# Expert weights of a hybrid decoder layer: nineteen slots in place of sixteen, filled in the order in which they come free, with the first pass over the experts written out

## The reference

```python
def hier_moe(h, w_rg, b_rg, w_re, b_re, w_e1, w_e3, w_e2):
    ...
    for gi in range(N_GROUPS):
        a = jnp.einsum('td,edf->tef', t, w_e1[gi])
        b = jnp.einsum('td,edf->tef', t, w_e3[gi])
        hid = jax.nn.silu(a) * b * gate[:, gi, :, None]
        y = y + jnp.einsum('tef,efd->td', hid, w_e2[gi])
    return y.reshape(B, S, D)
```

## Time and profile before

| | |
|---|---|
| median of 3 runs | 506.74 us (506.46 to 506.91) |
| the profiled execution | 506.75 us |
| its span, first to last instruction | 505.0 us |
| mean granted TensorE clock | 0.948 of full speed |
| TensorE matmuls busy | 426.5 us, 84% |
| VectorE, ScalarE, GpSimd busy | 159.5, 173.7, 157.3 us |
| moved by DMA | 163.19 MB, mean 323 GB/s |
| chain that ended last, by engine | PE 62%, DMA 24%, VectorE 4%, ScalarE 2% |

### The profile page before, as it was taken

The page is one execution under the profiler, slowest core; times in us unless marked ns, Lnnn a source line. Parts: engine busy times, 40 slices in busy tenths (PEclk is TensorE's granted clock), DMA queues, the critical chain, the costliest instruction groups (busy, mean ns, idle before and its releaser), DMA issues.

```text
span 505.0 us, 8937 instructions
## 1 busy us (share of the span) xinstructions
PE 426.5 (84%) x3772; PEld 319.0 (63%) x3772; DVE 159.5 (32%) x345; ACT 173.7 (34%) x305; POOL 157.3 (31%) x126
## 2 busy tenths in 40 slices
PE   1847998999999999999987989898849668594983
PEld 0415987999899999997965636354416244261541
DVE  0243304899692430455244011202110201102014
ACT  1235431853558276533452322130301102030122
POOL 0009894765936857997400000000000000000000
PEclk9969999998999999999997999999989979799798
DMA  8999979397598437558879699999999999999942
GB/s 295 392 364 388 281 242 387 123 342 244 182 355 257 165 112 262 185 194 287 332 286 422 254 392 424 420 421 421 420 422 421 424 422 422 422 420 422 423 197 85
DMA packets 55719, 163.19 MB, mean 323 GB/s; under 512 B 7058, under 2 KB 33924, under 8 KB 43268
## 3 DMA queue, kind: packets, MB, share of 16 engines
q1 hardware_dynamic: 50528, 159.53, 82.4%
q10 hardware_dynamic: 5156, 3.17, 2.1%
HBM read 161.64 MB, written 1.05 MB: 322 GB/s over the span
## 4 chain that ended last, share of the span: by engine, by line
PE 62%; DMA 24%; DVE 4%; SPq 3%; ACT 2%; issue 2%; POOL 1%; DVEq 0%; ACTq 0%
PE bank L1249 33%; DMA ring<-in_w_e 15%; PE bank L1558 8%; DMA mqk<-in_w_e 5%; PE bank L1570 4%; PE bank L1531 4%; DMA ring<-in_w_ada 4%; PE bank L1520 3%; PE bank L1202 3%; SPq L351 2%; SPq L339 1%; POOL ring_r L391 1%; PE bank L1604 1%; PE bank L1486 1%; ACT ring_r L426 1%
## 5 line engine op out<-in xcount | busy, mean ns | idle before, releaser
L391 POOL TENSOR_TENSOR ring_r<-ring,ring_r 128x512 fp32r<-128x512 f32 x120 | 156.9, 1345 | 87.8 <-ACT ring_r L426 87.6
L1249 PE MATMUL bank<-ring_r 128*128 128x256 f32 x832 | 111.3, 285 | 4.6 <-DVE att L815 2.3
L1249 PEld LDWEIGHTS bank<-ring_r 128*128 128x128 f32 x832 | 103.8, 191 | 7.3 <-issue 4.3
L648 ACT ACTIVATE raw<-bank,sm 128x128 f32<-128x128 f32 x72 | 27.1, 457 | 165.1 <-PE bank L1531 165.1
L426 ACT ACTIVATE ring_r<-ring 128x2048 fp32r<-128x2048 f32 x30 | 57.4, 1912 | 43.6 <-PE bank L1249 26.1
L1558 PE MATMUL bank<-ring,raw 128*32 128x256 f32 x768 | 51.9, 423 | 17.3 <-DMA ring<-in_w_e 16.9
L1558 PEld LDWEIGHTS bank<-ring,raw 128*32 128x32 f32 x768 | 28.3, 121 | 39.5 <-issue 27.8
L1127 DVE TENSOR_TENSOR tmp<-bank,tmp 128x256 f32<-128x256 f32 x8 | 3.4, 425 | 134.0 <-ACT tmp L656 134.0
L1531 PEld LDWEIGHTS bank<-const,xn 128*128 128x128 f32 x288 | 35.9, 199 | 9.0 <-issue 7.8
L1531 PE MATMUL bank<-const,xn 128*128 128x128 f32 x288 | 37.7, 286 | 1.1 <-DVE const L1078 1.1
L1202 PE MATMUL bank<-ring,sm 128*32 128x256 f32 x384 | 27.3, 434 | 12.3 <-DMA ring<-in_w_ada 12.3
(11 more groups left out here) (301 smaller groups left out, 533.3 us busy)
## 6 DMA issues: line engine op xcount, KB each, us to landing
ring<-in_w_e SPq DMA_DIRECT2D x72, 1024.0 KB, 25.9
ring<-in_w_ada SPq DMA_DIRECT2D x24, 1024.0 KB, 10.8
ring<-in_w_in SPq DMA_DIRECT2D x22, 1024.0 KB, 8.5
hT<-in_w_e SPq DMA_DIRECT2D x6, 1024.0 KB, 23.1
qkT<-in_w_e SPq DMA_DIRECT2D x6, 1024.0 KB, 25.1
gm<-in_w_e SPq DMA_DIRECT2D x6, 1024.0 KB, 26.3
mqk<-in_w_e SPq DMA_DIRECT2D x6, 1024.0 KB, 26.2
ring<-in_w_out SPq DMA_DIRECT2D x4, 1024.0 KB, 5.1
```

The lines of the kernel that those rows point to most:

```text
L391: pool.tensor_tensor(ring_r[:, slot_of(n), sl], ring[:, slot_of(n), sl], hi(d)[:, sl].bitcast(F32), ALU.subtract).then_inc(s["w_lo"], 1)
L648: ins = act.activation(xg[:, b, k, :], token_bank[:, j * P:(j + 1) * P], ACT.Identity, bias=S("B2p", KD)[:, k:k + 1], scale=S("A2p", KD)[: ...
L1249: ins = pe.matmul(out, left(k), right(k), start=(i == 0 and k == 0), stop=(i == 2 and k == nk - 1))
```

## The change

There are now nineteen slots. Two are a new tensor, `extra`; the SBUF for it comes from the reserve that the compiler object keeps for DMA descriptors (`dynamic_dma_scratch_size`), set from 16384 bytes per partition to 256. The third is the first 2048 floats of `late`, one tensor in which `osig` and most of `vaug` now lie; both are dead once `osig` has been transposed (job `ymT1`). A table `RELEASES` lists all nineteen with the job that frees each, in the order of those jobs, and the first nineteen expert units are put into the slots in that order (`ORDER`), as are all later ones. On SP the 77 further units of the first pass are now issued by straight code, unit m waiting for `used` >= m - 18, and on PE the eight quads are straight code, with constants in their waits. The further passes, which don't run here, use sixteen of the slots in loops.

```diff
-XSLOTS = SLOTS + 4
+XSLOTS = SLOTS + 7
+YSLOTS = 16
...
+def hi_slot(job):
+
+    return RING + [UNIT_JOB[n] for n in DENSE].index(job) % HI
+
+
+RELEASES = ([(SLOTS + 4, None), (SLOTS + 5, None), (SLOTS + 6, "ymT1"), (SLOTS + 1, "brm3")] + [((NPRE + u) % RING, "ada5") for u in range(4)] + [(SLOTS + 3, "merged")]
...
+               (SLOTS - 1, "wo3"), (SLOTS + 2, "wo3"), (SLOTS, "lgT")])
+ORDER = [i for i, _ in RELEASES]
...
-        vaug = sb("vaug", [TT, HEADS, P + 1])
-        osig = sb("osig", [TT, 512])
+        late = sb("late", [UNIT + TT * HEADS])
+        osig = late[:, 0:TT * 512].rearrange("p (t n) -> p t n", t=TT)
+        vaug = late[:, TT * 512:].rearrange("p (t h n) -> p t h n", t=TT, h=HEADS)
+        extra = sb("extra", [2, UNIT])
...
-            return n % RING if n < NPRE + RING else n - NPRE
+            return n % RING if n < NPRE else ORDER[(n - NPRE) % XSLOTS]
...
-            for m in range(XSLOTS):
-                sp.wait_ge(*last[m])
-                load(m // QU, m // QU, m % QU)
-            load_round(0, 0, XSLOTS)
-            with sp.Fori(1, NQ // LOOP) as r:
-                load_round(r, r * LOOP)
+            for m, (_, job) in enumerate(RELEASES):
+                if job == "merged":
+                    sp.wait_ge(s["merged"], 4)
+                elif job:
+                    sp.wait_ge(*full(job))
+                load(slot_of(NPRE + m), m // QU, m % QU)
+            for m in range(XSLOTS, NU):
+                sp.wait_ge(used, m - XSLOTS + 1)
+                load(slot_of(NPRE + m), m // QU, m % QU)
...
-            with pe.Fori(0, NQ // LOOP) as r:
-                for j in range(LOOP):
-                    quad(r, j)
+            for q in range(NQ):
+                quad(q // LOOP, q % LOOP)
...
-    nc = bacc.Bacc("TRN2", target_bir_lowering=False, num_devices=1)
+    nc = bacc.Bacc("TRN2", target_bir_lowering=False, num_devices=1, dynamic_dma_scratch_size=256)
```

More of the change, by code:

```diff
@@ L86 @@
 QU = len(QUAD_UNITS)
-XSLOTS = SLOTS + 4
+XSLOTS = SLOTS + 7
+YSLOTS = 16
 LOOP = 4
-assert LOOP * QU % XSLOTS == 0 and NQ % LOOP == 0
-TURNS = LOOP * QU // XSLOTS
+assert LOOP * QU % YSLOTS == 0 and NQ % LOOP == 0
+TURNS = LOOP * QU // YSLOTS
+NU = NQ * QU
 QUAD_POS = {u: i for i, u in enumerate(QUAD_UNITS)}
@@ L102 @@
 UNIT_JOB = unit_jobs()
+def hi_slot(job):
+    return RING + [UNIT_JOB[n] for n in DENSE].index(job) % HI
+RELEASES = ([(SLOTS + 4, None), (SLOTS + 5, None), (SLOTS + 6, "ymT1"), (SLOTS + 1, "brm3")] + [((NPRE + u) % RING, "ada5") for u in range(4)] + [(SLOTS + 3, "merged")]
+            + [((NPRE + 4) % RING, "wo0"), ((NPRE + 5) % RING, "wo1"), (hi_slot("wo1"), "wo1"),
+               ((NPRE + 6) % RING, "wo2"), (hi_slot("wo2"), "wo2"), ((NPRE + 7) % RING, "wo3"), (hi_slot("wo3"), "wo3"),
+               (SLOTS - 1, "wo3"), (SLOTS + 2, "wo3"), (SLOTS, "lgT")])
+ORDER = [i for i, _ in RELEASES]
+assert sorted(ORDER) == list(range(XSLOTS))
 DENSE_JOB = [UNIT_JOB[n] for n in DENSE]
@@ L303, in slot_of, with landed_total @@
         def slot_of(n):
-            return n % RING if n < NPRE + RING else n - NPRE
+            return n % RING if n < NPRE else ORDER[(n - NPRE) % XSLOTS]
         def landed_value(n):
             return 16 * sum(slot_of(m) == slot_of(n) for m in range(n + 1))
+        def landed_total(i):
+            return 16 * sum(slot_of(m) == i for m in range(NPRE + NU))
         def slot(i):
-            return ring[:, i, :] if i < SLOTS else (hT, qkT, gm, mqk)[i - SLOTS][:].rearrange("p a n -> p (a n)")
+            if i < SLOTS:
+                return ring[:, i, :]
+            if i < SLOTS + 4:
+                return (hT, qkT, gm, mqk)[i - SLOTS][:].rearrange("p a n -> p (a n)")
+            return (extra[:, 0, :], extra[:, 1, :], late[:, 0:UNIT])[i - SLOTS - 4]
         def unit(n, k):
@@ L343, in _, with load @@
                 sp.dma_start(unit(n, k), src[kind][:, :, c0:c0 + w]).then_inc(landed[slot_of(n)], 16)
-            def load(q, j, u):
+            def load(i, q, u):
                 w, e = QUAD_UNITS[u]
-                i = slot_of(NPRE + (j * QU + u) % XSLOTS)
                 expert = w_e[w][q * QUAD + e] if isinstance(q, int) else \
@@ L370, in _ @@
             with sp.If(over > 0):
+                sp.wait_ge(used, NU)
                 with sp.Fori(1, PASSES) as p:
                     with sp.Fori(0, NQ // LOOP) as r:
-                        load_round(p * (NQ // LOOP) + r, r * LOOP)
+                        for m in range(LOOP * QU):
+                            sp.wait_ge(used, (p * (NQ // LOOP) + r) * (LOOP * QU) + (m - YSLOTS + 1))
+                            load(ORDER[m % YSLOTS], r * LOOP + m // QU, m % QU)
             for tt in range(TT):
@@ L1545, in arrived @@
             def arrived(w, e, r, j):
[L1547 to L1550, removed]
+                m, k = j * QU + QUAD_POS[(w, e)], 2 if w == "w2" else 8
+                if isinstance(r, int):
+                    n = NPRE + r * (LOOP * QU) + m
+                    pe.wait_ge(landed[slot_of(n)], landed_value(n))
+                    return unit(n, k)
+                i = ORDER[m % YSLOTS]
+                first = landed_total(i) - 16 * TURNS * (NQ // LOOP)
+                pe.wait_ge(landed[i], r * (16 * TURNS) + (first + 16 * (m // YSLOTS + 1)))
+                return slot(i).rearrange("p (k n) -> p k n", k=k)
             def up(w, r, j, b):
```

## The result

The changed kernel takes **501.69 us** (median of 4 runs, 499.91 to 502.61), the kernel before 506.83 us beside it (4 runs, 506.46 to 508.95). The ratio is 0.9881, with a 95% interval of 0.9856 to 0.9906: faster by 1.2%; the medians lie 5.1 us apart. The forecast was 498.4 us, 8.35 us less than the profiled execution of before. The point is missed by 3.3 us. The ratio, put to the 506.74 us first shown, gives 500.7 us, within the range of 496.6 to 501.5; the median itself lies 0.2 us above it. The profiled execution took 500.96 us, with a span of 499.2 us and a mean granted clock of 0.951.

A forecast was written before the change was run, and what follows sets the result against it. Expert loads, 2.485 us each, were taken to bound the kernel from quad four on, after a DMA hole before quad one. Forecast: 506.75 - 7.45 - 0.3 - 0.6 = 498.4 us, range 496.6 to 501.5.

The forecast's parts named there:

- three more slots: Expert loads before quad one: nineteen land before the first wait for `used`, so load 88 lands 7.45 us earlier.
- new instruction fetches: PE's written-out quads five to eight: some six to eight new fetch packets, which do not slow the loads; 0.
- quad one's start: the branch: PE before quad one: written-out code removes the loop's branch and register instructions; 0.3 us off, between 0 and 0.39.
- quad one's start: the rest: Quad one starts near 280 us as before, since the router chain and not a load sets it; 0.
- clock of quad eight's w1 block: PE's last w1 block begins at another moment, so its lower-clock time lies between 5.17 and 6.49 us; 0.6 us off.
- tail behind that block: What PE and the tail do behind load 88, 37.6 us with that block; no change forecast for the rest.
- The rival: New fetches hold loads up: 0.9 us of one DMA engine each; 504.8 us if seven share an engine; chance 0.07.
- the mark against this step: Sign that the zero cost of fetches is wrong: loads after 370 us come more than 2.49 us apart.
- The order: Reordering slot filling: old order would start the stream 3.2 us later, still in time; 0 beyond filling the slots.
- Can PE use it?: PE's 6.32 us idle before quad five vanish, some 7 us remain before quad six; load 88's shift moves the end.
- The other rivals: Slots fill too late, 0.03; smaller reserve throttles loads, about 661 us, 0.03; clock stays up before quad eight, 496.2, 0.03.

The follow-up runs named there:

- out16: The changed kernel with sixteen slots in the old order and the old descriptor reserve, so only the first pass is written out; 508.21 us, ratio 1.0011.
- again: The changed kernel run once more with no edit; 501.41 us, ratio 0.9884 against the kernel before.
- warm: The changed kernel with ten needless matmuls on PE before quad eight's w1 block; 499.94 us, ratio 0.9839 against the kernel before.
- order19: The changed kernel with its nineteen slots filled in the old order, the three new ones last; 503.05 us, ratio 0.9897 against the kernel before.
- slots20: The changed kernel with a twentieth slot, made of `o` and part of `att` side by side; 497.27 us, ratio 0.9793 against the kernel before.
- slots20b: The same twenty-slot kernel as slots20, run once more; 498.10 us, ratio 0.9801 against the kernel before.
- reserve: The kernel before with only the descriptor reserve set to 256 bytes, loops kept; 508.06 us, ratio 1.0005.
- warm20b: The changed kernel with twenty slots, ten needless matmuls before quad eight's w1 block and three after its w3 block; 497.10 us, ratio 0.9796.

## Why the prediction was right and wrong

For the profiled pair, the sum by its terms:

| term | forecast | profiled pair |
|---|---|---|
| three more slots | -7.45 | -7.5 |
| new instruction fetches | 0 | +1.5 |
| quad one's start: the branch | -0.3 | -0.4 |
| quad one's start: the rest | 0 | +1.7 |
| clock of quad eight's w1 block | -0.6 | -0.8 |
| tail behind that block | 0 | -0.3 |
| sum | -8.35 | -5.8 (measured -5.79) |

*Three more slots* (with the order in which they are filled) was right, in size and in mechanism. From out16 to the changed kernel the lead time falls by 188.72 - 181.2 = 7.5 us, 3 x 2.485; the seventeenth slot alone gives 2.4, the twentieth 2.5. Each slot is one load's time until the hole is full. That the load with `used` >= 1 would follow a full set of slots held too, with 2.8 us to spare rather than 5.8. Of the 3.0 us that were lost 1.9 are a later last dense unit (230.09 in place of 228.21), which is the shift of the whole front part.

*The new fetches* is the step that failed. "In the stretch with two packets the loads moved as fast as in those without, so I take 0" averaged 23 us; a fetch delays one engine of 16, and whether it counts is decided at each one. The record of the kernel before already had such a case in that very stretch: a fetch begins at 303.6 us, and load 23 lands at 305.83, 3.46 us behind load 22. The rate of 422 GB/s doesn't show it. Two of the six from 370 us on counted in the changed kernel, by 0.52 and 1.06 us. The rival had the mechanism and the lower price, "A single packet that counts gives 499.3"; two of them give 500.2 by its own 0.9 us each. The landings from load 52 (371.71) to load 88 lie 90.99 / 36 = 2.53 us apart, beyond the 2.49 that the prediction had set as the mark against this step. The rule in the Trainium skill, "Runtime: NRT & Kernel Launch", section "Instruction fetch mechanics", is that the store is a FIFO with purely sequential prefetch, and that a taken branch outside its window forces a fetch; by it out16 would fetch no more than before. The trace disagrees again: 6 packets against 0 from 370 to 480 us, and 1.5 us with them. That a load's semaphore counts the engines one by one as each one's data lands stands in the Trainium skill, "DMA: Bandwidth & Descriptors", section "Why a DMA increments its semaphore by 16 and not by 1", and the trace agrees, since a single count behind the other fifteen makes the load late.

*The start of quad one.* "Quad one starts near 280 as before" took one execution's number for the kernel's. In the kernels that have the program of before up to that point it began at 280.24, 282.03 and 283.05 us, in the written-out ones between 280.27 and 283.89. The execution shown of before was the earliest of the thirteen in the table. The means, 281.8 of the three with loops and 281.8 of the ten written out, tell no gain from the branch, though the piece of 0.4 us did vanish from the chain in all ten; a spread of 3.6 us hides it. A difference within each execution tells it: from the issue of the last dense unit to the first w1 block it takes 51.96 to 52.26 us in the three with loops and 50.34 to 51.77 in all ten written out. Where the spread comes from is open; no experiment was made on it. The medians fit a start without a difference: the sum is then -7.5 + 1.5 - 0.6 - 0.3 = -6.9, and the medians of again and the kernel before beside it (6 and 23 runs) give -6.2, which by the interval of that ratio is good to some 1.7 us.

*The clock of the last w1 block* was right about the size that happens by itself, 5.71 and 6.10 us for the forecast 5.9, and warm shows the clock to be its cause: full clock and 3.66 us once the idle time before it is 1.05 us in place of over 5. Without the filler the block takes anything from 5.42 to 6.54 us in the seven written-out kernels of the table, so the term is known to half a us only, and that 0.6 came close to 0.8 is partly luck.

*The order* was cost at nothing beyond its part in filling the slots. "With the old order and nineteen slots the stream would start 3.2 us later and still be in time" was wrong: it counted the start of the stream and not the waits of the fifth to eighth load in it, one piece of the output projection each. order19 shows 2.1 us. It didn't spoil the sum, since the change has the new order; it would have spoiled the forecast of the slots alone.

*Can PE use it?* The idle time before quad five vanished, as forecast. Before quad six PE idled 3 us, not 7. Quad one began 1.3 us later, and the `down` blocks of quads three to five take 7.0 us at a granted clock of 0.74 (the piece at 343.47), where 5.4 was their time at full clock. PE is through with quad four at 374.6 and not at 370.2. It costs nothing because load 64, at 401.5, is still the later one. In slots20 load 64 lands at 399.9 and quad six begins at 400.0 with no idle time before it: with four slow `down` blocks before it in that execution PE had nothing left to give. In slots20b, with one slow block up to there, it idled 3.9 us before quad six, and the lead time was the same (178.70 and 178.74).

*The other rivals.* The reserve does nothing (ratio 1.0005), and the slots did not come too late. The measured time falls inside the range because the range had been given room for one or two fetches that count, and two is what came; the sum itself had none.

## What to carry to other kernels

A stream of loads that starves at one point gains one load's time for each buffer added, until the hole is full: count what must have landed and by when, and walk through every release on the way, not the first and the last. A free slot behind a waiting load in a queue is not free, so put buffers in the order of their release. Writing out a loop on an engine adds instruction fetches to the same 16 DMA engines that carry the data; in a kernel bound by loads compare the landings of single loads, since the mean rate does not show a late one. And take the start of a late stage from several executions before summing differences of a few us.

## What the runs showed of the hardware that was not expected

- A fetch of PE's instructions (16 KB, about 1.05 us in its own record) puts one of the 16 DMA engines back by about 1.55 us in a saturated stream, and a load of all 16 by anything from nothing to 1.36 us (load 60 of order19), as that engine had more or less head start. Of six in the stretch from 370 to 480 us two counted, in out16 and in the changed kernel.
- The second round of a loop of four quads fetched nothing in the kernel before and in reserve.
- The granted clock was 0.74 in `down` blocks that follow 1.59 and 0.52 us of idle time only, and the block took 7.0 us in place of 5.4. The blocks of quads one and two of the same execution, behind the same idle times, took 5.4 us (granted clock 1.00 from 320 to 327 us), so these idle times alone do not decide it. PE kept busy before one block had it at full clock and a later one slow.
- Executions with the same program ahead of it begin quad one up to 3.6 us apart (280.27 in warm20b, 283.89 in slots20b).
